# Following the conditioning chunks two by two in the first norm of a streaming encoder step

## The reference, cut to what matters

```python
sc = jax.nn.silu(c)
mod = sc @ w_ada[l] + b_ada[l]
sh1, sc1, g1, sh2, sc2, g2, sh3, sc3, g3 = jnp.split(mod, N_MOD, axis=-1)
hn = modulate(rmsnorm(x, norm_g[l, 0]), sh1, sc1)      # h * (1 + scale) + shift
x = x + 0.5 * g1[:, None, :] * swiglu(hn, ffn_w1[l, 0], ffn_w2[l, 0])
```

## Time and profile before

| what | us |
|---|---|
| median of three runs | 1526.99 |
| lowest, highest | 1525.47, 1527.32 |
| the profiled execution | 1524.26 |
| its span in the trace | 1522.6 |
| first 128x320 matmul of `plain_first` starts | 56.49 |
| first matmul of `plain_pair` 1 starts | 73.36 |

### The profile page before, as it was taken

How to read it: one execution, slowest core, us unless ns; L and a number is a source line. 1 busy time by engine, 2 the same in 40 slices (tenths; PEclk the granted TensorE clock), 3 DMA queues, 4 the chain that set the end, 5 groups by cost and what they waited for, 6 DMA issues and landing times.

```text
span 1522.6 us, 25593 instructions
## 1 busy us (share of the span) xinstructions
PE 1461.0 (96%) x10227; PEld 1398.0 (92%) x10227; DVE 1053.6 (69%) x1554; ACT 662.1 (43%) x1176; POOL 81.8 (5%) x143
## 2 busy tenths in 40 slices
PE   6799999999999999999889999999999999999996
PEld 4799999999999989988669999998999999999996
DVE  1667767676777776657885655756768687777866
ACT  3642534344334344566524452225525353434353
POOL 1400000000000030000010000004000000000003
PEclk8699999999999999999999999999999999999997
DMA  8552444426244512141172221263242222222312
GB/s 278 155 170 79 139 139 124 154 64 214 92 145 125 170 43 61 51 115 42 47 219 63 69 74 58 82 194 111 60 136 84 84 84 84 84 84 70 84 42 70
DMA packets 223466, 161.39 MB, mean 106 GB/s; under 512 B 5898, under 2 KB 209862, under 8 KB 223362
## 3 DMA queue, kind: packets, MB, share of 16 engines
q1 hardware_dynamic: 221666, 154.38, 34.2%
q0 software_dynamic: 1696, 5.56, 1.3%
HBM read 151.89 MB, written 8.03 MB: 105 GB/s over the span
## 4 chain that ended last, share of the span: by engine, by line
PE 83%; DVE 6%; ACT 3%; POOL 3%; DMA 3%; issue 1%; SPq 1%; ACTq 0%; DVEq 0%; POOLq 0%
PE acc L753 21%; PE acc L993 19%; PE pC L945 17%; PE acc L945 13%; PE acc L933 4%; PE pB L854 2%; DMA raw<-in_ffn_w 1%; PE pC L1120 1%; POOL hnf L703 1%; DMA ada_raw<-in_w_ada 1%; POOL hnf L702 1%; PE pB L815 1%; POOL hnf L698 1%; PE pC L1222 1%; PE pB L1111 1%
## 5 line engine op out<-in xcount | busy, mean ns | idle before, releaser
L1315 ACT ACTIVATE slot<-raw 128x512 fp32r<-128x512 f32 (+1 forms) x310 | 190.0, 617 | 246.2 <-PE acc L993 154.8
L993 PE MATMUL acc<-hid_hi,slot 128*128 128x320 f32 x1408 | 270.6, 310 | 4.4 <-DVE hid_lo L1961 3.7
L1807 DVE TENSOR_TENSOR slot<-raw,slot 128x512 fp32r<-128x512 f32 (+1 forms) x310 | 208.1, 675 | 51.1 <-ACT slot L1315 48.5
L993 PEld LDWEIGHTS acc<-hid_hi,slot 128*128 128x128 f32 x1408 | 221.6, 188 | 8.8 <-DVE hid_lo L1961 5.0
L945 PE MATMUL pC<-hn_hi,slot 128*128 128x320 f32 x912 | 216.3, 310 | 0.0
L753 PE MATMUL acc<-hn_hi,whi 128*128 128x320 f32 x688 | 166.6, 324 | 0.5 <-DVE hn_lo L1863 0.5
L993 PE MATMUL acc<-hid_lo,slot 128*128 128x320 f32 x704 | 161.4, 309 | 0.0
L945 PEld LDWEIGHTS pC<-hn_hi,slot 128*128 128x128 f32 x912 | 156.4, 188 | 2.5 <-issue 2.5
L753 PE MATMUL acc<-hn_hi,wlo 128*128 128x320 f32 x688 | 157.7, 311 | 0.0
L753 PE MATMUL acc<-hn_lo,whi 128*128 128x320 f32 x688 | 157.6, 311 | 0.0
L945 PE MATMUL acc<-tT,slot 128*128 128x320 f32 x912 | 146.8, 310 | 0.3 <-issue 0.3
(11 more groups left out here) (325 smaller groups left out, 2346.3 us busy)
## 6 DMA issues: line engine op xcount, KB each, us to landing
raw<-in_ffn_w SPq DMA_DIRECT2D x88, 512.0 KB, 5.2
sraw<-in_w_ada SPq DMA_DIRECT2D x26, 1024.0 KB, 7.7
wraw<-in_w_in SPq DMA_DIRECT2D x37, 512.0 KB, 3.8
raw<-in_ffn_w SPq DMA_DIRECT2D x16, 1024.0 KB, 5.1
ada_raw<-in_w_ada SPq DMA_DIRECT2D x8, 1024.0 KB, 12.0
wraw<-in_w_out SPq DMA_DIRECT2D x16, 512.0 KB, 4.0
raw<-in_ffn_w SPq DMA_DIRECT2D x8, 768.0 KB, 4.5
sraw<-in_w_ada_final SPq DMA_DIRECT2D x6, 1024.0 KB, 6.5
```

The source lines that it names most:

```text
L993: last = mm(half(a, h), w[t // 2][:, k, :], (hid_hi, hid_lo)[t % 2][:, k * TOK + h * HALF:k * TOK + (h + 1) * HALF], start=(k == 0 and t = ...
L1315: A(slot_as(fi, b, 0), source_of(fi, b), ACT.Copy).then_inc(blk_hi, 1)
L1807: V.tensor_tensor(out=slot_as(fi, b, 1), in0=source_of(fi, b), in1=slot_as(fi, b, 0).bitcast(F32), op=ALU.subtract).then_inc(blk_lo, 1)
```

## The change

Seven things are changed, all in the first norm and what feeds it.

- The chunks are taken in pairs, one of scales and one of shifts: order 0, 4, 2, 6, 1, 5, 3, 7 (`FIRST_CHUNK`). A pair covers two feature tiles, and tiles go in the order 0, 1, 4, 5, 2, 3, 6, 7 (`FIRST_TILE`).
- `plain_first(0)` does a pair's rows and columns, then those of the next pair, then the 24 matmuls of the first pair's two tiles, and so on.
- On DVE and ACT each pair has its own biases, scale, products, shift and split; the four blocks of weights are split after the first pair of tiles, not before the norm.
- r comes from the token rows: ACT squares each `x_row` with a sum along the row, five instructions, and takes one square root. The sums of squares on DVE and `mean_square(0)` fall away. `spread_r(0)` comes before the chunks.
- x is copied out of PSUM by DVE and not by ACT; ACT's exponential for `vecs` comes after r, and a one-element SiLU behind it.
- POOL multiplies the running streams' part of all eight tiles with r first, and does two operations a tile after that.
- Loads: c, x, small vectors, chunks s = 0, 1, the first pair's weights, chunks s = 2 to 7, the second pair's weights, then `load_duo(0)` once all chunks are multiplied (`ch_mm`, not `ch_tr`). Five chunk buffers; two of them lie where x was.

```diff
+FIRST_CHUNK = (0, 4, 2, 6, 1, 5, 3, 7)
+FIRST_RAW = (2, 3, 4, 0, 1, 2, 3, 4)
+FIRST_TILE = (0, 1, 4, 5, 2, 3, 6, 7)
...
+        def load_first(s):
+            m, r = FIRST_CHUNK[s], FIRST_RAW[s]
+            if r < 2:
+                sp.wait_ge(xt_tr, 2 * r + 2)
+                sp.wait_ge(tok_sq, 2 * r + 2)
+            elif s >= 3:
+                sp.wait_ge(ch_mm, FIRST_RAW.index(r) + 1)
...
+            if m == 0:
+                pool.wait_ge(xt_done, TT)
+                pool.wait_ge(rs_ready, 1)
+                for f in FIRST_TILE:
+                    st.done(nc.gpsimd.tensor_tensor(out=hn_f(f)[:, SEQ:TOK], in0=xT[:, f * TOK + SEQ:(f + 1) * TOK],
+                                                    in1=rT[:, SEQ:TOK], op=ALU.mult))
...
+        def first_chunks(q):
+
+            for s in (2 * q, 2 * q + 1):
+                wait(pe, ch_row, s - 1)
+                pe.wait_ge(ada_in[FIRST_RAW[s]], 16 * (1 + FIRST_RAW[:s].count(FIRST_RAW[s])))
+                cond_rows(s % 2, ada_raw[FIRST_RAW[s]])
+            for s in (2 * q, 2 * q + 1):
+                wait(pe, ch_sum, s - 1)
+                chunk_cols(0, s, s % 2, ada_row[s % 2])
...
+            if fi == 0:
+                first_chunks(0)
+            for j, k in enumerate(order):
+                odd, kk = divmod(k, KQ)
+                if fi == 0 and j % 2 == 0 and j < KD - 2:
+                    first_chunks(j // 2 + 1)
+                pe.wait_ge(hn_ready, 2 * fi * KD + j + 1)
...
+            for j, f in enumerate(order):
+                if fi == 0 and j % 2 == 0:
+                    for s in (j, j + 1):
+                        act.wait_ge(ch_mm, s + 1)
+                        wait(act, ch_tr, s - 1)
+                        A(ada_row[s % 2][:, :], ch_rows[s % 2], ACT.Copy).then_inc(ch_row, 1)
+                    biased(j)
...
+                if fi == 0 and j == 1:
+                    for b in range(4):
+                        blk(0, b)
...
         for c in range(TT):
+            act.wait_ge(x_in[c], 16)
+            A(hn_lo[:, 0:D_MODEL], x_row[c][:, :], ACT.Square, accum_out=rcol[:, c:c + 1]).then_inc(tok_sq, 1)
+            act.wait_ge(tok_sq, c + 1)
+        act.wait_ge(masks_done, 1)
+        A(rcol[:, :], rcol[:, :], ACT.Sqrt, bias=eps_t[:, 0:1], scale=1.0 / D_MODEL).then_inc(rms_sqrt, 1)
         copy_r(0)
+        act.wait_ge(vecs_in, 48)
+        st.done(A(vecs[:, 1, :], vecs[:, 1, :], ACT.Exp))
+        A(warm[:, :], eps_t[:, :], ACT.Silu)
...
+        def first_scale(q):
+
+            for s in (2 * q, 2 * q + 1):
+                dve.wait_ge(ch_tr, s + 1)
+                m = 2 * FIRST_CHUNK[s]
+                V.tensor_tensor(out=modc[:, m:m + 2, :], in0=ch_cols[s % 2].rearrange("p (f c) -> p f c", c=NSTR),
+                                in1=b_col[:, m:m + 2].unsqueeze(2).broadcast_to([P, 2, NSTR]), op=ALU.add
+                                ).then_inc(ch_sum, 1)
```

More of the change, by code:

```diff
@@ L145, in trunk_program @@
     tT = sb("tT", [P, KQ * 3 * TOK], F32R, reg)
+    slots += [sb(f"slot{i}", [P, 2 * WB], F32R, reg) for i in range(4, SLOTS - 1)]
+    sub = ExitStack()
+    c_row = sb("c_row", [NSTR, D_MODEL], stack=sub)
+    c_sil = sb("c_sil", [NSTR, D_MODEL], stack=sub)
+    b_row = sb("b_row", [MODT, P], stack=sub)
+    p_row = sb("p_row", [N_PAR, P], stack=sub)
+    ada_row = [sb(f"ada_row{i}", [P, ADA_COLS], stack=sub) for i in range(2)]
+    ada_raw += [sb(f"ada_raw{i}", [P, KD * ADA_COLS], stack=sub) for i in range(2, 5)]
+    sub.close()
     raw.append(sb("raw1", [P, 4 * WB], stack=reg))
@@ L214, in trunk_program @@
     xt_tr, xt_done = sem("xt_tr"), sem("xt_done")
-    ada_in = [sem(f"ada_in{i}") for i in range(ADA_RING)]
+    ada_in = [sem(f"ada_in{i}") for i in range(len(ada_raw))]
     s_in = [sem(f"s_in{j}") for j in range(2)]
@@ L884, in chunk_cols @@
             last.then_inc(ch_tr, 1)
-        def first_rows(m):
-            pe.wait_ge(ada_in[m % ADA_RING], 16 * (m // ADA_RING + 1))
-            cond_rows(m % 2, ada_raw[m % ADA_RING])
-        for m in range(ADA_FIRST + 1):
-            if m == ADA_FIRST:
-                mean_square(0)
-            if m < ADA_FIRST:
-                wait(pe, ch_row, m - 1)
-                first_rows(m)
-            if m:
-                wait(pe, ch_sum, m - 2)
-                chunk_cols(0, m - 1, (m - 1) % 2, ada_row[(m - 1) % 2])
@@ new lines, in plain_first @@
+        def plain_first(fi):
+            g = fi * NB
+            order = [j // 2 + KQ * (j % 2) for j in range(KD)] if fi else FIRST_TILE
+            if fi == 0:
[5 more added lines that the diff above has]
+                pe.wait_ge(hn_ready, 2 * fi * KD + j + 1)
+                for d in range(2):
+                    if kk == 0:
+                        pe.wait_ge(blk_lo, g + 2 * d + odd + 1)
+                    whi_, wlo_ = (slot_of(fi, 2 * d + odd, lo, WB)[:, kk * P:(kk + 1) * P] for lo in range(2))
+                    for t, (w, a) in enumerate(((whi_, hn_hi), (whi_, hn_lo), (wlo_, hn_hi))):
+                        for h in range(2):
+                            last = mm(half(acc[d], h), w, a[:, k * TOK + h * HALF:k * TOK + (h + 1) * HALF],
+                                      start=(j == 0 and t == 0), stop=(j == KD - 1 and t == 2))
+                            if j == KD - 1 and t == 2:
+                                last.then_inc(blk_done, 1)
@@ L1503, in ffn @@
                         hi(d - 5)
-                    act.wait_ge(sq_added, squares + d)
+                    wait(act, sq_added, squares + d)
                     if d == KD - 1:
@@ L1828, in norm_ffn @@
             dve.wait_ge(rinv_ready, m + 1)
-            prod(0)
-            prod(1)
-            for j in range(KD):
-                f = j // 2 + KQ * (j % 2)
-                if j + 2 < KD:
+            if fi:
+                prod(0)
+                prod(1)
+            for j, f in enumerate(order):
+                if fi == 0 and j % 2 == 0:
+                    first_scale(j // 2)
+                    prod(j)
+                    prod(j + 1)
+                if fi and j + 2 < KD:
                     prod(j + 2)
```

208 lines of the change are left out of this document (78 added, 130 removed).

## The result

| | before | after |
|---|---|---|
| median of the runs made together, us | 1526.23 (1524.7 to 1527.32, 4 runs) | 1509.13 (1507.3 to 1510.41, 4 runs) |
| the profiled execution, its span | 1524.26, 1522.6 | 1509.9, 1508.3 |
| first 128x320 product | 56.49 | 33.37 |
| `plain_pair` 1 starts | 73.36 | 56.94 |
| from there to the end of the span | 1449.2 | 1451.4 |

The direction and most of the mechanism were right: pair 1 starts 16.4 us earlier, not 11.2. The sizes of several steps were wrong, and so was what the first product waits for: the stream of chunks, not ACT.

A forecast was written before the change was run, and what follows sets the result against it. The body was taken as PE-bound, the start as led by chunk loads, the norm's serial tail and products. Steps put pair 1 at 62.2 instead of 73.4 us, 11.2 less: 1527.0 to 1516, range 1511 to 1522.

The forecast's parts named there:

- the clock does not fall in the chunk phases: Rival, chance 0.18: the clock falls between product groups, second and third pair take 5.6 us each, time 1519.7.
- it is not low throughout: Rival, chance 0.08: bursts too short to raise the clock, all of `plain_first` at 1.2 GHz, time 1529.8.
- that the loads bind: Rival, chance 0.10: small vectors or a late-freed buffer hold the chunk stream up some 5 us, time 1521.
- The two chunk phases between the products: Rows, a copy and columns of the third and last chunk pairs, between product groups: 4.2 us each.
- The chain to the first pair's columns: From the start through r, table loads and the first two chunks: both columns at 26.4 us.
- the step that let ACT's serial chain set the first product: Before the first product: ACT's splits and row copies lead, loads cost 0, products start at 36.0 us.
- From there to the end of the blocks: From both first columns at 26.4 us, through the first two tiles, to ACT's four weight blocks split at 33.6.
- The columns of the second pair: On PE ahead of the first products, after ACT copies the rows at 34.4 us: done at 36.0.
- First group and last group: First 24 products take 5.6 us, starting at the low clock; the last group waits for low parts, ending at 62.1.
- better case: Chance 0.08: clock rises sooner, saving 2.3 us in the first pair, and x's copy is 0.5 shorter: time 1513.
- more than 1 us of growth between pair 1 and the end: Sign against the forecast: about 1449 us from pair 1 to the span's end should stay within 1 us.
- lost afterwards: Rival, chance 0.06: the gain at 62 us is lost later to something paced by a load, time 1525 to 1528.

The follow-up runs named there:

- e2: Changed kernel with the exponential and its two table loads moved to the end of the first SwiGLU, one-element SiLU left out; median 1508.63 us, ratio 0.9888.
- e6: e2 with the three small vector loads also issued behind the second pair's weights; median 1507.04 us, ratio 0.9875.
- e5: The changed kernel run again with no edit; median 1510.28 us, ratio 0.9905.
- e11: Kernel before the change, with three useless fp32 matmuls on PE behind the spread of r; median 1525.68 us, ratio 1.0003.
- e12: Changed kernel with r taken from the feature tiles again and its spread behind the first two chunks' rows; median 1518.55 us, ratio 0.9955.
- e4: Changed kernel with PE, DVE and ACT all taking every chunk before the first tile is normed; median 1521.06 us, ratio 0.9973.
- e3: Changed kernel with PE alone taking all chunks before the first product, other engines still pairwise; median 1515.15 us, ratio 0.9935.
- e1: Changed kernel with the small vectors loaded ahead of x again; median 1510.64 us, ratio 0.9914.
- e7: Changed kernel with three useless fp32 matmuls on PE behind the second chunk's columns; median 1504.79 us, ratio 0.9862.
- e13: e9 with three more useless matmuls behind the third chunk's row, and POOL multiplying only two tiles before the first pair; median 1504.39 us, ratio 0.9871.
- e9: Changed kernel with the edits of e6 and e7 together; median 1507.55 us, ratio 0.9882.

## Why the prediction was right in direction and wrong in size

**What was right.** That only the start of pair 1 counts and its shift arrives at the end: 16.4 at pair 1, 17.1 in the medians. The order of the chain, the four groups, the first group's 5.6 (5.5 in the trace) with the clock turning inside it, the last group waiting for its low part (0.95) and ending 8.5 after the last columns (8.4). The squares are hidden, and r is early. The loads further on were hidden. Three rivals are out: the clock does not fall in the chunk phases, it is not low throughout, and nothing is lost to a load later (below). The remaining one, that the loads bind, is half right: the stream does set the start, but 2.6 earlier than ACT was forecast to, and so costs nothing against the forecast. The Trainium skill's page "TensorE: Matmul & The Clock Gate", section "HAM oscillation — how this bites in real kernels", has bursts that each start at the low clock after a wait for data; here the phases between bursts are filled with matmuls, not waits, and the granted clock is 1.00 through all of 37.2 to 56.9.

**What was wrong.** Three steps of the forecast failed. The two chunk phases between the products, priced at 4.2 each, took 3.0: 2.4 of the 5.2 us. The chain to the first pair's columns, 26.4, ended at 24.6, and the chain from there to the end of the blocks was shorter again. And the step that let ACT's serial chain set the first product, with the loads at 0, had the wrong wait: the fourth chunk sets it. Pair 1 was forecast at 62.1 and came at 56.94. The 5.2 us are terms of the sum:

- Both first columns, -1.8. The transposes end at 16.86, not 17.6: 40 take 7.3 and not 8.0, because I scaled the first 32 of before, and most of those ran at half the pace of the last. The spread takes 0.73, not 1.3: its row was one at the low clock, and at 18 us the clock is high. The columns take 0.74 a chunk, not 1.0, since they come in one go and the clock is high for the first 0.5 us of them.
- From there to the end of the blocks, -1.1: 6.1 and not 7.2. The four blocks take 2.17 and not 2.5, ACT's two high parts 1.35 and not 1.46, DVE's two products 1.56 and not 1.84 (the same two of the next pair take 1.81, which no run explains); the rest are shorter gaps between the engines.
- The columns of the second pair, +0.3: they waited for the fourth chunk and not for ACT. The forecast took the loads at 0 and ACT as the bound; the fourth chunk did land inside its 28 to 32 (29.64), but ACT had split the blocks at 30.7, not at 33.6. So the two bounds stand 0.8 apart, and e2 and e6 show which leads: ACT's chain moved by 1.65 moves nothing; the stream moved by 1.75 moves the product by 1.75.
- The two chunk phases, -2.4: 3.0 each and not 4.2. In the rows, before: 1.07 a row at the high clock and 32 columns' matmuls of 363 ns each. The phase needs 1.86 for two rows and 1.1 for eight column matmuls at the high clock, ACT's copy of the first row beside the second. I had added the copy and low-clock columns to high-clock rows.
- First group and last group, -0.2 together.

The transposes of x on PE, before and after (shortest/median/longest ns):

```profile
L834 PE MATMUL acc<-ident,x_row x40: 272/421/477, 11.5 to 18.9; 128*128 128x128 f32 x40
L857 PE MATMUL acc<-ident,x_row x40: 272/286/473, 9.6 to 16.6; 128*128 128x128 f32 x40
```

PE waits for nothing inside either group of 32 or 24. Transposes start 0.21 us apart up to about 17.0 before and 13.3 after, and 0.11 apart from there: a factor of two, as between the clock's two levels. The views print a granted clock of 1.00 for both stretches, but the trace's records of the clock only begin at those moments, so in the first 13 to 17 us the pace is to be trusted and not the 1.00.

Most of these terms, those of PE above all, have one source: durations from rows at the lower clock or the slower pace were used for a stretch in which PE runs at 2.4 GHz. On ACT and DVE the rows were means of operations that mostly stood apart, and the new ones stand back to back. They err on one side and so add up. Two slips carry no weight: the clock rose 4.8 us after the first product before, not 4.5, and pair 1 is at 62.1 in the steps and at 62.2 in the sum. The forecast's "better case" named the mechanism (an earlier clock, a short copy) but sized it at 2.8.

**What took 2.2 back.** The forecast said that more than 1 us of growth between pair 1 and the end would speak against it. It grew by 2.2 in the profiled execution (1449.2 to 1451.4), but by 0.5 in e5, the same program. Counted from pair 1, DVE's operations begin at the same time in both traces 656 us behind it, and 2.7 us apart at 695. The same work between these two points, before and after:

```profile
729.40:768.20 38.80, 30.06 (x235) 21.88 (x235) 30.52 (x39) 21.95 (x37) 5.12 (x6) 1.00 0.28 82
```

```profile
713.00:754.40 41.40, 33.74 (x235) 24.71 (x233) 30.43 (x38) 22.38 (x37) 5.12 (x6) 0.87 0.28 82
```

The 235 matmuls, the other engines' busy time and the transfers are as before; PE is busy 3.7 us longer, at a mean granted clock of 0.87 instead of 1.00. From there to the end some 0.5 come back. So the rival "lost afterwards" isn't what happened: the time goes to dips of the clock, and not to a load. In the middle of the layer, where PE works with pauses, the clock dips for some microseconds at a time, and where it does differs between executions. e11, whose program behind the start is that of before, ends 3.8 later (1453.0) at the same start of pair 1, 2.7 of it around a dip near 1130 that the trace of before doesn't have. Over all traces the part behind pair 1 scatters by 5 us (1447.9 to 1453.0), with or without the change. Why the dips fall in one execution and not in the next stays open; no run was made for it.

**How the gain divides.** Undone one at a time: r from the token rows is worth 11.4 at pair 1 (e12), the pairwise order with the place of the blocks 13.1 (e4), of which PE's order alone is 3.3 (e3), the order of the loads 2.2 (e1). They overlap, and their sum is more than the 16.4. By the ratios of the medians the same four are worth some 9, 12, 6 and 3 us, each to within 3 to 4. The copy of x on DVE, POOL's new order and the earlier `load_duo(0)` were never undone alone, so their share is open.

## What to carry to other kernels

Take a duration from a row only at the clock and in the spacing that it will have in the new place: look up the granted clock of both stretches first, and where the work moves from a stretch at 1.2 GHz to one at 2.4, work out the sum at both. Where two chains end close together (here the fourth chunk's row at 31.7 and ACT's copy of the third at 31.0), one run that moves each apart costs little and says which one to shorten. Useless matmuls are worth trying where PE waits for data right before its dense work; here they helped where they reached nearly up to it (e7, e13), and not or hardly where 2 us and more of waiting remained (e11, e9).

## What the runs showed of the hardware that I had not expected

- **In two runs the clock was high before the dense work because PE was kept busy.** In e7 2.34 us of useless fp32 matmuls ahead of a chunk's row had the clock at 2.4 GHz at 28.6, 4 us before the first product; in e13 it never fell. Followed by 2.37 us of waiting the same matmuls did nothing (e11); in e9, with PE busy 1.62 of 3.80 us behind them, the clock held until 28.5 (26.1 in e6) and fell before the products. Each is one execution. Behind chunk work, during which the clock had stayed low for 14 us before with PE busy 12.28 us, it rose in e3 at 43.8 (11.76 of 13.80 us busy) and in e4 at 45.0; what makes the difference stays open.
- **The moment of the rise differs between executions of one program:** 37.2 and 39.5 us, worth 0.9 in the first group.
- **Three small broadcast loads** (64 bytes for each of 128 partitions) in front of the chunks cost the stream 1.75 us (28.04 in e6 against 29.79 in e2), their issue or their transfer.
- **A table load costs its 1.28 us here and no more:** two of them and two small operations take from 19.76 to 22.78. The Trainium skill's page "ScalarE: Activation LUTs", section "What ACT_TABLE_LOAD costs", adds a drain of about 1.38 us to each; the trace shows none.
